# A one-layer decoder step on one core: seventeen products of ones instead of ten ahead of the input's first tile

## The chip, the cores and the metric

The kernel runs on one core of one Trainium2 chip. The metric is the device time of one launch in microseconds (us), less being better. TensorE (PE) multiplies matrices, VectorE (DVE) and ScalarE (ACT) work on elements, GpSimd (POOL) fills constants and starts some transfers, SyncE (SP) starts the large transfers. Each engine runs its own queue of instructions in order and waits on semaphores that the others raise. A row of the trace also tells TensorE's granted clock, which stands at one of two levels: 1.00 is 2.4 GHz, 0.50 is 1.2 GHz.

## The reference

One step of one decoder layer, for 256 prompt tokens and 8 x 4 sampled tokens (288 tokens in all), in float32:

```
u = RMSNorm(x) @ W_in                    # 2048 -> 5632, split between two head groups
x = x + concat([HGRN2(A), SWA(B)]) @ W_out
x = x + SwiGLU(RMSNorm(x))               # 2048 -> 5632 -> 2048
```

The layer also returns the new keys, values and recurrent states. The part that matters here is the very start: `x` (token rows of 2048) must stand transposed (2048 rows in 16 tiles of 128, 288 tokens in columns) and scaled by the norm's weights, before the first product with `W_in` can be made.

## The kernel before

All weights pass through the core in slabs of 1 MB (128 x 2048 float32). SP loads a slab into one of three buffers `raw`; ACT rounds it to `wh` (function `high`, line 646, semaphore `high_done`), DVE forms the rest `wl = raw - wh` (function `low`, line 1002, `low_done`). The activations are split in the same way into `act_h` and `act_l`. PE then makes three products for each slab and each of 16 tiles: `wh*act_h`, `wh*act_l`, `wl*act_h`. For the first slab they are made in an order that follows the arrival of the operands (`passes_as_they_come`): 16 of `wh*act_h` (line 1577), 16 of `wl*act_h` (line 1580), 16 of `wh*act_l` (line 1583). From the second slab on, function `passes` interleaves them (lines 1563, 1564, 1567). There are 44 slabs for `W_in`, 16 for `W_out`, 132 for the feed-forward part.

What comes ahead of the first slab:

- POOL fills `ones` (128 x 128) at line 489. SP starts the transfers of the small constants and of `x` in five pieces: first columns 0 to 1023 of the two prompt blocks, then the whole of the sampled tokens (`x_sample`, 32 rows), then columns 1024 to 2047 of the prompt blocks. The slabs of `W_in` stand behind them in the same queue.
- PE waits for `ones` and makes ten products of `ones` with `ones` (`warm(10)`, line 1527). Their result goes to a bank that is overwritten later and nobody reads it.
- PE waits for the constants and the norm's weights, transposes the weights (line 1532), and makes ten more products of ones.
- PE transposes `x`: for each tile k of 16, three transpositions (line 1513): prompt block 0, prompt block 1, sampled rows. Tile 0 waits for each of the three pieces before its transposition. The results go to six PSUM slots in turn; from tile 6 on, PE waits until tile k-6 has been taken away.
- ACT takes a tile as `act_h[k]` (line 664) and copies the even tiles to `reg_x` (line 667); DVE makes `act_l[k]` (line 1019) and copies the odd ones (line 1023). ACT rounds slab 0 behind tile 9 and slab 1 behind tile 15, DVE makes the rest of slab 0 behind tile 9.
- PE transposes the other parameters (line 1538) and goes on with slab 0.

The order on each engine is the order in which the code is written; there is no planner.

Of the kernel before, what the change touches and what calls it, by code (L numbers as in the profile page):

```python
# [123 lines left out]
def layer_kernel(nc, x_prompt, x_sample, cache_k, cache_v, state_hgrn, norm_mix, w_in, lower_bounds, hgrn_norm,  # L124
# [13 lines left out]
    with ExitStack() as ctx:  # L138
# [1362 lines left out]
        def _(pe):  # L1501
# [23 lines left out]
            def warm(n):  # L1525
                for _ in range(n):
                    mm(mx[:, 0, 0:P], ones, ones, start=True, stop=True)
# [2 lines left out]
            pe.wait_ge(small_in, 16)  # L1530
            pe.wait_ge(gain_in, 16)
            nc.tensor.transpose(acc[3][:, 0:KD], param_rows[0:KD], ident[0:KD, 0:KD]).then_inc(gain_t, 1)
            warm(10)
            for k in range(KD):
                x_transpose(k)
            pe.wait_ge(gain_done, 1)
# [674 lines left out]
```

## Time and profile before

| | us |
|---|---|
| median of 3 runs (1355.39 to 1356.23) | 1355.54 |
| time of the profiled execution | 1357.95 |
| span of the profiled execution, first to last instruction | 1356.1 |
| PE busy in the span | 1348.2 (99%) |
| mean granted clock of TensorE | 0.992 |

The profile is of one execution, whose time is 2.41 us above the median of the runs. The span lacks 1.85 us of that execution's time, which lie outside the first and last instruction. A row of a timeline gives start, duration, engine, line, operation, output<-inputs, shapes and how many instructions of the kind were merged into the row (x20). A product in float32 shows as two matrix instructions, a transposition or a product of rounded operands as one.

### The profile page before, as it was taken

The numbers are of one execution on the slowest core, as the hardware profiler recorded it, in microseconds if no ns is written. First come the engines' busy times: TensorE is split into PE (matmuls) and PEld (weight loads), VectorE is DVE, ScalarE is ACT, GpSimd is POOL, SyncE is SP. The second block draws the span as 40 slices with busy tenths as digits, with TensorE's granted clock in tenths as the row PEclk, the third lists the DMA queues.
The fourth block names the chain that finished last, engine by engine and source line by source line (L and its number), as shares of the span: only waits on it lengthen the run. The fifth ranks groups of instructions, "written<-read, shape, count | busy, mean of one in ns | idle before, by whom it ended". The sixth has DMA issues, their size and how long they took to land.

```text
span 1356.1 us, 25313 instructions
## 1 busy us (share of the span) xinstructions
PE 1348.2 (99%) x11094; PEld 1312.7 (97%) x11094; DVE 772.7 (57%) x1006; ACT 533.5 (39%) x617; POOL 114.3 (8%) x153
## 2 busy tenths in 40 slices
PE   9999999999999999999999999999999999999998
PEld 7999999988999999999999999999999999999998
DVE  5346765699638475455454645555554555555464
ACT  6347975432344244333323333332333333332331
POOL 2010430214100440000000000000000000000000
PEclk7999999999999999999999999999999999999999
DMA  9796545557844546556565555556555555655552
GB/s 276 198 311 172 165 133 149 137 162 203 256 156 143 173 136 186 158 172 168 156 176 166 156 158 184 156 156 173 170 157 162 179 156 168 165 165 156 169 173 71
DMA packets 321082, 231.43 MB, mean 171 GB/s; under 512 B 5175, under 2 KB 292736, under 8 KB 320651
## 3 DMA queue, kind: packets, MB, share of 16 engines
q1 hardware_dynamic: 314768, 206.19, 52.9%
q0 software_dynamic: 6112, 23.59, 5.5%
q8 instruction: 88, 1.44, 0.4%
q14 instruction: 24, 0.19, 0.0%
q10 hardware_dynamic: 90, 0.02, 0.0%
HBM read 219.99 MB, written 14.97 MB: 173 GB/s over the span
## 4 chain that ended last, share of the span: by engine, by line
PE 98%; DMA 1%; ACT 0%; DVE 0%; SPq 0%; issue 0%; DVEq 0%
PE acc L1563 30%; PE acc L1567 30%; PE acc L1564 29%; PE mx L1769 1%; PE mx L1513 1%; DMA reg_qkf<-in_x_sample_dram 1%; PE mx L1681 0%; PE mx L1653 0%; PE mx L1860 0%; PE mx L1668 0%; PE mx L1833 0%; PE acc L1577 0%; PE mx L2085 0%; PE mx L1895 0%; PE acc L1513 0%; PE acc L1580 0%
## 5 line engine op out<-in xcount | busy, mean ns | idle before, releaser
L1563 PE MATMUL acc<-act_h,wh 128*128 128x288 f32 x2208 | 597.0, 299 | 0.0
L1564 PE MATMUL acc<-act_l,wh 128*128 128x288 f32 x2208 | 593.7, 295 | 0.0
L646 ACT ACTIVATE wh<-raw 128x2048 fp32r<-128x2048 f32 x192 | 366.7, 1910 | 241.9 <-PE acc L1567 230.6
L1002 DVE TENSOR_TENSOR wl<-raw,wh 128x2048 fp32r<-128x2048 f32 x192 | 440.1, 2292 | 7.6 <-PE acc L1583 3.9
L1563 PEld LDWEIGHTS acc<-act_h,wh 128*128 128x128 f32 x2208 | 415.5, 188 | 5.9 <-issue 5.0
L1564 PEld LDWEIGHTS acc<-act_l,wh 128*128 128x128 f32 x2208 | 414.7, 188 | 0.1
L1567 PE MATMUL acc<-act_h,wl 128*128 128x288 f32 x2208 | 321.7, 298 | 0.0
L1567 PEld LDWEIGHTS acc<-act_h,wl 128*128 128x128 f32 x2208 | 301.7, 189 | 5.0 <-issue 3.8
L1563 PE MATMUL acc<-mix_h,wh 128*128 128x288 f32 x832 | 228.3, 299 | 0.0
L1564 PE MATMUL acc<-mix_l,wh 128*128 128x288 f32 x832 | 227.7, 295 | 0.0
L1563 PEld LDWEIGHTS acc<-mix_h,wh 128*128 128x128 f32 x832 | 157.1, 189 | 1.7 <-issue 1.7
L1564 PEld LDWEIGHTS acc<-mix_l,wh 128*128 128x128 f32 x832 | 156.2, 188 | 0.0
L1567 PE MATMUL acc<-mix_h,wl 128*128 128x288 f32 x832 | 142.3, 296 | 0.0
L1489 DVE TENSOR_TENSOR reg_x<-acc,reg_x 128x288 f32<-128x288 f32 x176 | 79.2, 455 | 104.7 <-PE acc L1567 104.7
L1567 PEld LDWEIGHTS acc<-mix_h,wl 128*128 128x128 f32 x832 | 120.3, 188 | 0.0
L952 ACT ACTIVATE reg_t<-reg_t 128x288 f32<-128x288 f32 x44 | 19.7, 447 | 185.2 <-DVE reg_t L1454 185.2
L1454 DVE TENSOR_TENSOR reg_t<-acc,reg_t 128x288 f32<-128x288 f32 x44 | 20.1, 457 | 126.3 <-PE acc L1567 126.3
L955 ACT ACTIVATE mix_h<-reg_t 128x288 fp32r<-128x288 f32 x44 | 19.6, 447 | 179.0 <-DVE reg_t L1462 179.0
L1462 DVE TENSOR_TENSOR reg_t<-acc,reg_t 128x288 f32<-128x288 f32 x44 | 20.1, 457 | 119.1 <-PE acc L1567 119.1
L1350 DVE TENSOR_TENSOR reg_x<-acc,reg_x 128x288 f32<-128x288 f32 x32 | 14.3, 453 | 37.5 <-PE acc L1567 37.5
L1456 DVE TENSOR_TENSOR reg_t<-reg_t 128x288 f32<-128x288 f32 x44 | 20.2, 458 | 22.6 <-ACT reg_t L952 22.6
L1466 DVE TENSOR_TENSOR mix_l<-reg_t,mix_h 128x288 fp32r<-128x288 f32 x44 | 20.2, 458 | 22.6 <-ACT mix_h L955 22.6
(284 smaller groups left out, 714.3 us busy)
## 6 DMA issues: line engine op xcount, KB each, us to landing
raw<-in_w_in_dram SPq DMA_DIRECT2D x44, 1024.0 KB, 6.0
raw<-in_w_gate_dram SPq DMA_DIRECT2D x44, 1024.0 KB, 5.6
raw<-in_w_up_dram SPq DMA_DIRECT2D x44, 1024.0 KB, 5.6
raw<-in_w_down_dram SPq DMA_DIRECT2D x44, 1024.0 KB, 5.1
raw<-in_w_out_dram SPq DMA_DIRECT2D x16, 1024.0 KB, 5.3
reg_x<-in_state_hgrn_dram POOLq DMA_DIRECT2D x16, 256.0 KB, 4.8
out_dram<-reg_x POOLq DMA_DIRECT2D x16, 256.0 KB, 3.6
bias_rows<-bias_line POOLq DMA_DIRECT2D x1, 3072.0 KB, 18.3
```

Source lines behind the costliest of these rows:

```text
L646: nc.scalar.activation(wh[:, s % WH, :], raw[:, s % RAW, :], ACT.Copy).then_inc(high_done, 1)
L952: nc.scalar.activation(tmp[:, 2 + t % 2, :], tmp[:, t % 2, :], ACT.Silu).then_inc(gate_silu, 1)
L955: nc.scalar.activation(mix_h[:, FC * (c % 2) + t, :], tmp[:, 4 + t % 2, :], ACT.Copy)\
L1002: nc.vector.tensor_tensor(wl[:, s % WL, :], raw[:, s % RAW, :], wh[:, s % WH, :].bitcast(F32), ALU.subtract).then_inc(low_done, 1)
L1454: nc.vector.tensor_tensor(tmp[:, t % 2, :], ps, rstd2, ALU.mult).then_inc(gate_scaled, 1)
L1456: nc.vector.tensor_tensor(tmp[:, 2 + t % 2, :], tmp[:, 2 + t % 2, :], rstd2, ALU.mult)\
L1462: nc.vector.tensor_tensor(tmp[:, 4 + t % 2, :], ps, tmp[:, 2 + t % 2, :], ALU.mult)\
L1466: nc.vector.tensor_tensor(mix_l[:, slot, :], tmp[:, 4 + t % 2, :], mix_h[:, slot, :].bitcast(F32), ALU.subtract)\
L1489: nc.vector.tensor_tensor(xT[:, m, :], acc[n][:, 0:T], xT[:, m, :], ALU.add)\
L1563: mm(out, w_h[:, i, cols], a_hi[:, place(i), :], start=(i == 0), stop=False)
L1564: mm(out, w_h[:, i, cols], a_lo[:, place(i), :], start=False, stop=False)
L1567: ins = mm(out, w_l[:, i, cols], a_hi[:, place(i), :], start=False, stop=(i == k - 1))
```

## The change

The second batch of products of ones, between the transposition of the norm's weights and the transposition of the first tile of `x`, is made longer by seven. Nothing else differs, and no wait, transfer or buffer is touched.

```diff
             pe.wait_ge(small_in, 16)
             pe.wait_ge(gain_in, 16)
             nc.tensor.transpose(acc[3][:, 0:KD], param_rows[0:KD], ident[0:KD, 0:KD]).then_inc(gain_t, 1)
-            warm(10)
+            warm(17)
             for k in range(KD):
                 x_transpose(k)
```

The order of PE's instructions at the start of the program follows, as a difference (- before, + after; `mx<-reg_a` is the product of ones, `acc<-small,reg_a` the transposition of the norm's weights, `mx<-small,reg_qkf` those of `x`):

```order
 L1527 MATMUL mx<-reg_a 128x128 x10
 L1532 MATMUL acc<-small,reg_a 128x16
-L1527 MATMUL mx<-reg_a 128x128 x10
+L1527 MATMUL mx<-reg_a 128x128 x17
 L1513 MATMUL mx<-small,reg_qkf 128x128 x2
 L1513 MATMUL mx<-small,reg_qkf 128x32
```

Seven products of ones, which are 14 matrix instructions in the trace, now stand ahead of the first transposition of `x`. The order on the other four engines is unchanged.

## Rows read from the trace of the kernel before

**Rows 1.** The page: busy time of the engines, and the chain that ended last
```profile
PE 1348.2 (99%) x11094; PEld 1312.7 (97%) x11094; DVE 772.7 (57%) x1006; ACT 533.5 (39%) x617; POOL 114.3 (8%) x153
PE 98%; DMA 1%; ACT 0%; DVE 0%; SPq 0%; issue 0%; DVEq 0%
```

**Rows 2.** Waits of PE over the whole span: who for whom, us, times, longest
```profile
PE mx L1513 <- DMA reg_qkf<-in_x_sample_dram: 1.3, 1, 1.3
PE mx L1527 <- POOL reg_a L489: 1.0, 1, 1.0
PE mx L2103 <- DVE reg_x L1489: 0.6, 1, 0.6
PE mx L1513 <- DMA reg_qkf<-in_x_prompt_dram: 0.5, 1, 0.5
PE mx L1681 <- ACT reg_x L750: 0.2, 1, 0.2
```

**Rows 3.** Timeline of PE: start us, us, engine, line, operation [idle before <-releaser]
```profile
1.00 4.04 PE L1527 MATMUL mx<-reg_a 128*128 128x128 f32 x20 [1.00 <-POOL reg_a L489]
5.13 2.50 PE L1527 MATMUL mx<-reg_a 128*128 128x128 f32 x20
7.47 0.27 PE L1513 MATMUL mx<-small,reg_qkf 128*128 128x128 f32 x1
8.20 0.33 PE L1513 MATMUL mx<-small,reg_qkf 128*128 128x128 f32 x1 [0.46 <-DMA reg_qkf<-in_x_prompt_dram]
9.85 2.19 PE L1513 MATMUL mx<-small,reg_qkf 32*128 32x32 f32 x10 [1.32 <-DMA reg_qkf<-in_x_sample_dram]
...
22.30 0.33 PE L1538 MATMUL acc<-small,reg_a 43*128 43x43 f32 x1
22.55 4.21 PE L1577 MATMUL acc<-act_h,wh 128*128 128x288 f32 x16
26.56 3.01 PE L1580 MATMUL acc<-act_h,wl 128*128 128x288 f32 x16
29.41 2.29 PE L1583 MATMUL acc<-act_l,wh 128*128 128x288 f32 x16
31.54 0.29 PE L1563 MATMUL acc<-act_h,wh 128*128 128x288 f32 x1
```

**Rows 4.** Stretches: busy us (instructions) of PE, PEld, DVE, ACT, POOL; clock; DMA
```profile
1.30:3.90 2.60, 2.60 (x13) 2.60 (x13) 0.00 (x0) 0.00 (x0) 0.00 (x0) 1.00 0.74 208
5.50:7.40 1.90, 1.90 (x20) 1.90 (x19) 0.00 (x0) 0.07 (x1) 0.00 (x0) 1.00 1.00 281
9.00:10.00 1.00, 0.15 (x1) 0.13 (x1) 0.00 (x0) 0.00 (x0) 0.00 (x0) 1.00 0.94 332
11.00:12.00 1.00, 1.00 (x6) 0.57 (x5) 0.90 (x3) 1.00 (x3) 0.00 (x0) 0.55 1.12 321
11.10:22.30 11.20, 11.20 (x41) 6.05 (x40) 9.44 (x18) 9.94 (x22) 3.45 (x7) 0.50 1.18 287
28.00:29.00 1.00, 1.00 (x8) 1.00 (x8) 0.00 (x0) 1.00 (x2) 0.88 (x3) 0.92 0.83 350
246.00:250.00 4.00, 4.00 (x121) 2.55 (x123) 0.00 (x0) 0.13 (x1) 0.00 (x0) 1.00 1.10 267
250.00:253.40 3.40, 3.40 (x28) 3.06 (x28) 0.00 (x0) 0.60 (x1) 1.97 (x1) 0.50 0.00 0
```

**Rows 5.** Timeline of PE's weight loads for `x`, one row a tile
```profile
9.85 0.37 PEld L1513 LDWEIGHTS mx<-small,reg_qkf 32*128 32x128 f32 x3 [1.51 <-DMA reg_qkf<-in_x_sample_dram]
10.39 0.37 PEld L1513 LDWEIGHTS mx<-small,reg_qkf 32*128 32x128 f32 x3 [0.17 <-issue]
...
14.31 0.53 PEld L1513 LDWEIGHTS mx<-small,reg_qkf 32*128 32x128 f32 x3 [0.33 <-issue]
15.17 0.53 PEld L1513 LDWEIGHTS mx<-small,reg_qkf 32*128 32x128 f32 x3 [0.33 <-issue]
```

**Rows 6.** The chain that ended last, in order of time: start us, us, what
```profile
22.62 4.14 PE acc L1577 x16
...
29.57 2.13 PE acc L1583 x16
```

**Rows 7.** Timeline of PE: products of 288 columns
```profile
35.81 2.30 PE L1567 MATMUL acc<-act_h,wl 128*128 128x288 f32 x16
...
246.26 0.29 PE L1564 MATMUL acc<-act_l,wh 128*128 128x288 f32 x1
...
250.63 3.64 PE L1567 MATMUL acc<-act_h,wl 128*128 128x288 f32 x16
```

**Rows 8.** Timelines of ACT and DVE around slab 0
```profile
19.44 0.49 ACT L664 ACTIVATE act_h<-acc,gains 128x288 fp32r<-128x288 f32 x1
...
20.50 0.52 ACT L664 ACTIVATE act_h<-mx,gains 128x288 fp32r<-128x288 f32 x1
...
22.40 0.50 ACT L664 ACTIVATE act_h<-mx,gains 128x288 fp32r<-128x288 f32 x1
22.80 1.90 ACT L646 ACTIVATE wh<-raw 128x2048 fp32r<-128x2048 f32 x1
...
18.21 0.45 DVE L1023 COPY reg_x<-mx 128x288 f32<-128x288 f32 x1
19.57 2.29 DVE L1002 TENSOR_TENSOR wl<-raw,wh 128x2048 fp32r<-128x2048 f32 x1 [0.92 <-ACT wh L646]
...
24.22 0.93 DVE L1019 SCALAR_TENSOR_TENSOR act_l<-mx,gains,act_h 128x288 fp32r<-128x288 f32 x2
```

**Rows 9.** The issue of slab 0 of `W_in` on SP: time from issue to landing
```profile
L448 SPq DMA_DIRECT2D raw<-in_w_in_dram x1: 787/787/787, 4.1 to 4.1; - x1
DMA to landing us min/median/max: 11.7/11.7/11.7
```

## The prediction

> **What bounds the kernel now.** I read the page first. PE is busy for 1348.2 of 1356.1 us, and the chain that ended last runs over PE for 98% of the span [rows 1]. So the time is the sum of PE's own work: it becomes shorter only if PE idles less, or if its work runs at a better clock. The waits come second. All waits of PE that the trace names add up to 3.6 us, and 1.8 of them stand at the start: 0.5 us for the second prompt block of `x` and 1.3 us for the sampled rows [rows 2]. The third view is PE's timeline over the first 32 us [rows 3]: the second batch of ones begins at 5.13, the first transposition of `x` at 7.47, the second at 8.20, the third at 9.85 with the landing of `x_sample`, and from there PE has no gap. The last view is the granted clock by stretches [rows 4]. PE is nearly idle from 9 to 10 us (0.15 us busy). During the second at 11 to 12 us the clock falls (0.55 on average), it is 0.50 from 11.10 to 22.30, and it comes back in the second from 28 to 29 (0.92, so that it rises at about 28.1). Hence PE works some 17 us at half speed. A tile of `x` takes 0.54 us (9.85 to 10.39) at the full clock and 0.86 us (14.31 to 15.17) at half [rows 5]. Sixteen products of 288 columns take 4.14 us at half and 2.13 us at full by the chain of waits [rows 6], 0.259 and 0.133 us each.
>
> **The products themselves.** The change removes nothing and adds seven products. The ten of the second batch take from 5.13 to 7.47, 0.234 us each [rows 3]. Seven take 7 x 0.234 = 1.64 us and end at 9.11 in place of 7.47. The first two transpositions follow without a wait (0.27 and 0.33 us by their rows, counted in full though they overlap): 9.71. The third can't start before `x_sample` lands at 9.85, as now. So the added work lies wholly in the gap, with 0.14 us to spare, and costs nothing. The cover is the landing of `x_sample`; if it landed earlier than 9.71, each tenth would be paid. Behind PE stand ACT and DVE, which wait for tile 0 as a whole and get it at the same time. No transfer is issued by PE, and none waits for it here.
>
> **What the clock does.** That is the other, less certain term. The clock fell after a stretch in which PE had waited from 7.74 to 8.20 and from 8.53 to 9.85, 1.8 us in all. In the changed kernel PE has dense products of ones until 9.11 and waits for 0.14 us. The clock was full throughout the batch of ones (20 instructions in 1.90 us, against 13 in 2.60 us in the first batch before it had risen; the clock column shows 1.00 there only because the trace holds no earlier step) [rows 4]. From the last dense product to the fall it now takes 11.1 - 7.5 = 3.6 us, and at the second place where it fell (below) about the same: the last product of a slab ends at 246.5, the clock is low at 250.0 [rows 4, 7]. The last dense product moves to 9.1, which gives a fall at 12.7 for the same distance. The transpositions that follow without a gap may hold the clock for longer; I allow the distance once more, 16.3, and take the middle, 14.5. The gain at each:
>
> - At 12.7: 1.6 us more at full, 3.0 tiles in place of 1.9, 1.1 x 0.86 = 0.95 us won by the transpositions.
> - At 14.5: 3.4 us, 6.3 tiles in place of 4.0, 2.3 x 0.86 = 2.0 us won. PE would be done with the parameters at 20.6 and not at 22.55.
> - At 16.3: 5.2 us, 9.6 tiles in place of 6.0, 3.6 x 0.86 = 3.1 us, as far as DVE follows.
>
> Does something else hold PE back? Tile 15 needs DVE's copy of tile 9, done at 18.66; tile 15 would start at about 19.4. Slab 0 is rounded by 19.5 (the rest of it starts at 19.57), `act_h[15]` is made at 22.90, the rest of slab 0 at 21.86, and the last `act_l` at 25.15 [rows 8]. Even if ACT and DVE gained nothing, PE needs `act_h[15]` at 24.4, the rest of slab 0 at 24.7 and the last `act_l` at 27.5 or later. So PE keeps the 2.0 us up to the first slab.
>
> With 2.0 us won, the first slab's products begin at 20.6 and 16 at half speed end at 24.7. Now the rise decides. (a) If it stays at 28.12: 3.4 us at half give 13.2 of the next 16 products, 2.8 x 0.133 = 0.4 us more, then 2.13: 30.65 in place of 31.54, a gain of 0.9 us. (b) If it comes as long after the first dense product as now (28.12 - 22.55 = 5.6 us), at 26.2: 5.8 products at half, 10.2 x 0.133 = 1.36, then 2.13: 29.7, a gain of 1.85 us. (c) If it comes as long after the first dense product as at the second place, where the products begin at 250.63 and the clock is back at 253.4, 2.8 us [rows 4, 7], it comes at 23.4: 10.8 products at half, 5.2 x 0.133 = 0.7, then twice 2.13: 28.4, a gain of 3.2 us. With the fall at 12.7 about half of these remain, 0.5 to 1.6; with the fall at 16.3 some half more. I take (b), 1.85 us, near the middle of 0.9 and 3.2.
>
> **A second place.** The clock is also 0.50 from 250.0 to 253.4, behind 4.00 us in which PE was fully busy with small products [rows 4]. Sixteen products take 3.64 us there and 2.30 us elsewhere [rows 7], a price of 1.3 us. When everything lies 2 us earlier this may vanish or not: 0 to 1.3 us. I put it at zero in the sum and keep it for the range.
>
> The profiled execution took 1357.95 us, so it would come to 1356.1. It stood 2.41 us above the median of the runs, though; half-speed stretches are the one thing in the trace that could differ that much, so the median may lack part of what is to be won. I still take the same 1.85 us off the median: 1355.54 - 1.85 = 1353.7.
>
> **Two rules of the Trainium skill.** The record shows PE 100% busy from 11.10 to 22.30, 11.20 us, with the clock at 0.50 all the time, and fully busy from 246 to 250 with the clock at 0.50 behind it [rows 4]. The Trainium skill's page "TensorE: Matmul & The Clock Gate", section "What's actually happening", says that the gate follows how busy the array has been recently. If "busy" were what the rows call busy, the clock would have come back among the transpositions; the trace doesn't bear that reading out, and transpositions seem to weigh little. By that reading the sum would be that of rival 2.
>
> The same page of the Trainium skill, in the same section, warns that the number of slow products varies from run to run with the moment at which a kernel starts, and advises not to fit to a count of them. No row here can show it, since there is one execution. By that rule the sum for the median would be near nothing, rival 1.
>
> **The rivals.**
>
> 1. *The median doesn't move.* The clock falls where it did, since seven products aren't enough to hold it, or it falls and rises at other moments in most executions, so that the gap mattered only in the profiled one. For it: the 2.41 us between profile and median. Against it: the clock fell right behind the only idle stretch at the start, and three runs within 0.84 us leave little room for a clock that changes at other moments each time. Time: 1355.5, with up to 0.3 us either way.
> 2. *The clock stays full throughout the transpositions.* ACT then sets the pace: tile 0 at 10.2, two tiles in 1.06 us (19.44 to 20.50) [rows 8], ten tiles by 15.5; slab 0 lands at 4.1 + 11.7 = 15.8 [rows 9], is rounded by 17.7, six tiles more by 21.0. PE ends the 16 first products at 21.1, and 4.26 us later, at 25.4, the slab: 6.1 us won, 1349.4. Against it: 11.20 us of pure transpositions never brought the clock back.
> 3. *Slower: the seven are made at half speed.* A product of ones takes 0.40 us before the rise (2.60 us for 13 instructions, two a product) [rows 4]. Were the clock still low in the second batch, it would last until 5.13 + 17 x 0.40 = 11.9, two transpositions go to 12.5, and tile 0 is 2.6 us late; ten would have ended in time. Time: 1355.54 + 2.6 = 1358.1. It decides from the first product that is slow beyond the 0.14 us of room, at 0.17 us each. Against it: in the profile the clock was up before the second batch.
>
> **How the numbers follow.** A change within 0.2% (2.7 us) is about what a measurement of this kernel can't tell from none. Chances: the forecast case 0.58 (gain 0.5 to 3.2 us, with the second place up to 4.5), rival 1 0.33, rival 2 0.03, rival 3 0.06. Of the forecast case about 0.15 lies beyond 2.7 us, where (c) holds or the second place is added. With rival 2: faster 0.19, same 0.76, slower 0.05 (a part of rival 3 is smaller than 2.7 us). The range reaches from 1351.4 (the forecast case with 4.1 us) to 1356.0 (rival 1 with a little loss); about 0.15 lies outside.
>
> **What the profile would show.** PE's second batch is 34 instructions from 5.13 to about 9.1, the wait for the second block is gone, and that for `x_sample` is under 0.3 us. The granted clock is 1.00 until 12.7 or later, tiles come every 0.54 us until then, L1577 begins near 20.6 and L1563 near 29.7. The forecast is wrong if the clock falls at 11.1 again, if the second batch ends after 9.5, or if PE starts to wait for ACT or DVE among the tiles.

## The result

The changed kernel takes 1351.91 us (median of 8 runs, 1351.41 to 1353.1), the kernel before 1356.2 us in the same measurement (median of 8 runs, 1355.39 to 1357.93). The ratio is 0.9972, with a 95% interval of 0.9959 to 0.9984: faster by 0.28%, which is clear of no change. The forecast of 1353.7 us was 1.8 us too high, inside the range (1351.4 to 1356.0), but the step that gave it was not the one that took place.

The page of the changed kernel, busy time of the engines:

```profile
PE 1342.5 (99%) x11108; PEld 1309.2 (97%) x11108; DVE 772.2 (57%) x1006; ACT 532.6 (39%) x617; POOL 116.3 (9%) x153
```

PE makes 14 more matrix instructions than in [rows 1] and is busy for 5.7 us less: the same work ran at a better clock. The span is 1350.0 us where it was 1356.1, and the mean granted clock 1.000 where it was 0.992. PE's timeline over the start, to be laid beside [rows 3]:

```profile
1.00 4.62 PE L1527 MATMUL mx<-reg_a 128*128 128x128 f32 x20 [1.00 <-POOL reg_a L489]
5.55 0.23 PE L1532 MATMUL acc<-small,reg_a 16*128 16x16 f32 x1
5.72 4.06 PE L1527 MATMUL mx<-reg_a 128*128 128x128 f32 x34
9.62 2.18 PE L1513 MATMUL mx<-small,reg_qkf 128*128 128x128 f32 x12
...
18.23 0.25 PE L1538 MATMUL acc<-small,reg_a 43*128 43x43 f32 x1
18.42 2.43 PE L1577 MATMUL acc<-act_h,wh 128*128 128x288 f32 x15
21.14 0.40 PE L1577 MATMUL acc<-act_h,wh 128*128 128x288 f32 x1 [0.29 <-ACT act_h L664]
21.39 2.28 PE L1580 MATMUL acc<-act_h,wl 128*128 128x288 f32 x16
23.50 2.30 PE L1583 MATMUL acc<-act_l,wh 128*128 128x288 f32 x16
25.64 0.29 PE L1563 MATMUL acc<-act_h,wh 128*128 128x288 f32 x1
```

The products of ones and the transpositions follow each other without a gap. The transpositions end at 18.2 (22.3 before), slab 1 begins at 25.64 (31.54 before): 5.9 us earlier. The stretch of transpositions, for [rows 4] (busy us and instructions of PE, weight loads, DVE, ACT, POOL; granted clock; DMA):

```profile
11.10:18.20 7.10, 7.10 (x40) 4.37 (x40) 6.48 (x16) 6.97 (x16) 3.45 (x7) 1.00 1.19 296
246.00:250.00 4.00, 4.00 (x98) 3.58 (x97) 1.49 (x6) 2.03 (x3) 2.91 (x2) 1.00 0.00 0
250.00:253.40 3.40, 3.40 (x28) 3.40 (x27) 3.40 (x5) 1.40 (x6) 0.00 (x0) 1.00 0.02 5
```

The clock is 1.00 all through them; forty instructions take 7.10 us, against 11.20 us for 41 in [rows 4]. The second half-speed stretch, at 250 us, is absent as well (1.3 us by [rows 7]). Part of this goes into new waits. PE's waits over the span:

```profile
PE mx L1527 <- POOL reg_a L489: 1.0, 1, 1.0
PE mx L1611 <- ACT reg_t L685: 0.8, 1, 0.8
PE mx L2103 <- DVE reg_x L1489: 0.6, 1, 0.6
PE mx L1769 <- issue: 0.4, 1, 0.4
PE acc L1577 <- ACT act_h L664: 0.3, 1, 0.3
```

The waits for `x` of [rows 2] are gone. PE now waits 0.3 us for ACT's last tile, as it no longer runs slowly enough to be always behind, and 0.8 us for ACT at the squares of a head group (line 1611). 5.9 won at the start, 1.3 at 250 us, 0.8 and 0.4 given back at lines 1611 and 1769 make 6.0 of the 6.1 us between the spans.

So the two profiles differ by 6.1 us and the two medians by 4.3. Two questions are left: why these differ, and what holds the clock.

### The profile page after: what moved, and what is told of

The parts are those of the page before. It is cut to its first block, busy times and chain, and to the rows that moved or that the text cites. A ratio compares the mean times of both kernels' runs of the same rounds, so it can differ in the third digit from the quotient of the medians.

```text
span 1350.0 us, 25341 instructions
## 1 busy us (share of the span) xinstructions
PE 1342.5 (99%) x11108; PEld 1309.2 (97%) x11108; DVE 772.2 (57%) x1006; ACT 532.6 (39%) x617; POOL 116.3 (9%) x153
## 4 chain that ended last, share of the span: by engine, by line
PE 96%; DMA 2%; ACT 1%; DVE 0%; issue 0%; SPq 0%; DVEq 0%
PE acc L1563 30%; PE acc L1567 30%; PE acc L1564 29%; DMA raw<-in_w_in_dram 2%; PE mx L1769 1%; PE mx L1681 0%; PE mx L1653 0%; PE mx L1860 0%; PE mx L1668 0%; PE mx L1833 0%; PE mx L2085 0%; PE mx L1895 0%; PE mx L1810 0%; PE mx L1698 0%; PE mx L1705 0%
```

## Experiments

Each set of three or four kernels ran with the kernel before on the same chip, 12 executions a kernel and 29 or 35 of the kernel before; the three sets ran on three different chips. Every execution tells its mean granted clock. I sort them in two groups: 0.998 and more, called held, and 0.997 and less, called fallen (most of these have 0.992 to 0.995). In the first two sets of the kernel before no value lies between 0.995 and 0.998; in the third three of 29 do (0.996 once, 0.997 twice, 1354.83 to 1357.02 us), and they are counted as fallen. That the line tells a clock held at the start from one that fell there is shown by the profiled executions alone, each of which agrees with it. A held execution can still have a short stretch at half speed elsewhere.

| kernel | filler, where | held | median us | median held | median fallen |
|---|---|---|---|---|---|
| before, set 1 | 10 products | 8 of 35 | 1355.95 | 1351.97 | 1356.71 |
| nine transpositions | 10 + 9 transpositions | 6 of 12 | 1354.57 | 1352.43 | 1356.97 |
| 17, then an idle wait | 17 | 0 of 12 | 1359.53 | | 1359.53 |
| 24 products | 24 | 12 of 12 | 1352.73 | 1352.73 | |
| 14 products | 14 | 7 of 12 | 1353.44 | 1353.13 | 1356.94 |
| before, set 2 | 10 | 8 of 35 | 1355.84 | 1351.01 | 1356.38 |
| fifteen transpositions | 10 + 15 transpositions | 10 of 12 | 1352.46 | 1352.35 | 1354.10 |
| six in the middle of tile 0 | 10 + 6 | 11 of 12 | 1352.70 | 1352.62 | 1355.14 |
| seven in the first batch | 17 + 10 | 12 of 12 | 1352.74 | 1352.74 | |
| 17 products again | 17 | 12 of 12 | 1352.35 | 1352.35 | |
| before, set 3 | 10 | 7 of 29 | 1355.83 | 1351.16 | 1356.21 |
| 27 products | 27 | 11 of 12 | 1354.36 | 1354.17 | 1358.27 |
| 12 products | 12 | 3 of 12 | 1355.84 | 1350.68 | 1356.14 |
| 12 ahead, 5 in the middle | 12 + 5 | 11 of 12 | 1353.08 | 1352.94 | 1353.87 |

The first measurement of the changed kernel adds 8 of 8 held. This answers the first question. **The kernel before is a mixture**: in 23 of 99 executions the clock holds and the median time is 1351 to 1352, in 76 it falls and the median time is 1356.2 to 1356.7, about 5 us more. The change doesn't make a held execution faster. It makes nearly all executions held ones. The share of fallen ones, 76 of 99, times 5.0 us is 3.8 us, less what the products themselves cost. The first measurement of the kernel before has no clock beside its eight times, but all are 1355.39 us or more, above every held execution of the table's kernel before (1353.87 at most): by their times all eight are fallen, which explains why its difference, 4.3 us, is larger than in the sets.

### Filler of another kind

```diff
             warm(10)
+            for _ in range(9):
+                nc.tensor.transpose(mx[:, 0, 0:P], ones, ident)
             for k in range(KD):
```

> The gap ahead of the sampled rows is filled with nine transpositions of the ones tile (0.17 to 0.20 us each at the full clock, about 1.6 us) in place of the seven products of ones. Theory A (an idle gap lets the clock fall, any work that fills it holds the clock): as the changed kernel, clock 1.00 throughout, 1352 us, L1563 begins near 25.6. Theory B (only dense products of ones hold it; transpositions weigh too little): the clock falls near 11 us as before, 1355.5 to 1356.5 us. Theory C (chance: clock steps lie elsewhere in each execution): a mixture, 1352 to 1356.

Held in 6 of 12, ratio 0.9993 (0.9974 to 1.0011), not told apart from before. This was undecided: nine transpositions were shorter than I had counted. PE's timeline of this kernel (line 1535 is the filler), in an execution whose clock held:

```profile
5.24 2.50 PE L1527 MATMUL mx<-reg_a 128*128 128x128 f32 x20
7.58 1.15 PE L1535 MATMUL mx<-small,reg_a 128*128 128x128 f32 x9
8.56 0.57 PE L1513 MATMUL mx<-small,reg_qkf 128*128 128x128 f32 x2
10.00 1.87 PE L1513 MATMUL mx<-small,reg_qkf 32*128 32x32 f32 x10 [0.88 <-DMA reg_qkf<-in_x_sample_dram]
```

They took (8.56 - 7.58) / 9 = 0.109 us each and left 0.88 us idle. So fifteen were tried in the next set, `range(15)` in place of `range(9)`:

> In the last set nine transpositions took only 0.109 us each and left 0.9 us of idling; the clock held in 6 of 12 executions. Fifteen of them behind the ten products fill the gap to about 9.1 us, as seven products of ones do. Theory A (only the idle time ahead of the landing matters, whatever the work is): held in all or nearly all executions, median 1352. Theory B (the kind of work matters, dense products hold the clock and transpositions hold it less well): still a mixture, a quarter or more of the executions with the clock at 0.995 or less and 1355 to 1359 us.

Held in 10 of 12, ratio 0.9984 (0.9971 to 0.9998). Filling the gap with transpositions does nearly what filling it with products does; the two others have a mean clock of 0.996 and 1354.0 and 1354.2 us, so they were at half speed for less time than most fallen executions of before; where, no profile shows. Theory A gives the main effect. Whether the kind of work matters a little besides is left open by 10 of 12 against 20 of 20.

### An idle wait behind the seventeen

```diff
                     if k % 8 == 0 and k // 8 < len(x_in[j]):
                         pe.wait_ge(x_in[j][k // 8], 16)
+                    if k == 0 and j == 2:
+                        pe.wait_ge(x_in[1][1], 16)
```

> The changed kernel with seventeen products, but the third transposition of tile 0 also waits for the last piece of x (lands near 12.1 us), so that PE idles some 2.2 us behind the products. Theory A: the clock falls in the idle stretch or right behind it and the gain is lost: about 1356.2 plus up to 2.2 for the later tile 0, 1356.5 to 1358.5 us, clock 0.50 during most of the transpositions. Theory B (seventeen dense products are what holds the clock): clock 1.00, only the direct 2.2 us are lost: about 1354 us.

1359.53 us, ratio 1.0025 (1.0012 to 1.0038); no execution of 12 held. Stretches of this kernel:

```profile
11.00:12.00 1.00, 0.00 (x0) 0.00 (x0) 0.00 (x0) 0.00 (x0) 0.00 (x0) 1.00 1.15 315
12.00:13.00 1.00, 0.86 (x6) 0.64 (x6) 0.00 (x0) 0.54 (x2) 0.33 (x1) 1.00 1.19 291
13.00:14.00 1.00, 1.00 (x5) 0.49 (x4) 0.64 (x2) 1.00 (x3) 1.00 (x3) 0.52 1.19 289
14.00:24.00 10.00, 10.00 (x37) 5.44 (x36) 8.12 (x15) 8.68 (x20) 2.12 (x5) 0.50 1.02 244
```

PE idles for 1.88 us until 12.14, the clock falls in the second from 13 to 14 (0.52 on average), and ten microseconds of transpositions without a gap don't bring it back. Seventeen products don't protect against a gap behind them. The time is above my upper end (1358.5): it lies 2.8 us above the fallen executions of before (1356.71), of which 2.3 are the lateness of tile 0 (12.14 against 9.85). In its profile PE has two more waits that the kernel before doesn't have [rows 2], 0.8 us together, which are enough for the rest:

```profile
PE mx L1613 <- ACT reg_t L685: 0.5, 1, 0.5
PE mx L1771 <- issue: 0.3, 1, 0.3
```

### The same delay without idling

To take the delay apart from the clock, `warm(27)` in place of `warm(17)`:

> Twenty-seven products: the batch and two transpositions end near 12.1 us, so tile 0 is as late as in the kernel with the wait for the last piece of x (third transposition at 12.14), but PE isn't idle. Theory A: held in all executions; only the direct price of the later tile 0 is paid, at most 2.2 us: 1353 to 1354.5 us, 5 to 6 us below the 1359.5 of the kernel with the idle wait. If the lateness of tile 0 itself made the 1359.5: as slow, 1358 or more.

Tile 0's third transposition comes later still than in the kernel with the wait (12.45 + 0.33 = 12.8 against 12.14), and yet the time is 1354.36 us, 5.2 us less, in another set whose kernel before has nearly the same median (1355.83 against 1355.95); 11 of 12 held where I had expected all (the other has 0.997). The kernel with the wait differs in that PE idles. So the idle stretch costs 5 us through the clock, and lateness alone costs 2.0 us (1354.36 - 1352.35, in two sets) for some 2.2 us of lateness against seventeen (12.8 against 10.6 in the profile shown below). Its ratio to before is 0.9993 (0.9981 to 1.0005): with ten products more, the kernel can't be told apart from the one before.

### More and fewer products

`warm(24)`, `warm(14)` and `warm(12)`:

> Twenty-four products in the second batch. All theories: the clock stays full. The batch ends 7 x 0.112 x 2 = 1.6 us after that of seventeen, at 10.7 to 11.3, so tile 0 is complete about 1.2 to 1.5 us later. If ACT and the landing of slab 0 at 15.9 had room, less of it is lost; by the rows ACT takes up slab 0 without a wait behind tile 9, so I expect 1.0 to 1.5 us above seventeen: 1353.0 to 1353.5 us.

> Fourteen products: four of the seven, so 0.9 us of the 1.8 us of idling stay. Theory A: about half the idling; the clock is held in many executions but not in all: 1352 to 1356 us with a wide spread. Theory B (a count of dense products): nearly as seventeen, 1352 to 1353 us. If the gap must vanish entirely, 1356 us.

> Twelve products, 0.45 us of the gap filled. Shares of held executions so far: ten 8 of 35 twice, fourteen 7 of 12, seventeen 20 of 20. I expect the share to grow with the filled time: 4 to 6 of 12, median near 1355.5. As few as ten gives would say that there is a threshold between twelve and fourteen.

Twenty-four: held in 12 of 12, 1352.73 us, 0.4 to 0.8 above seventeen where I had expected 1.0 to 1.5; ratio 0.998 (0.9966 to 0.9993). Fourteen: 7 of 12, ratio 0.9988 (0.9971 to 1.0005). Twelve: 3 of 12 where I had expected 4 to 6, ratio 1.0002 (0.9986 to 1.0019), the share of ten. The share of held executions rises from a quarter at ten and twelve to about half at fourteen and to all at seventeen, 20 of 20. With 12 executions a share is known to about a quarter, so where exactly it bends isn't settled, but it rises with how much of the gap is filled, and the executions of a kernel differ. In the profiled execution of twelve products the clock held and PE's products and transpositions had no wait for `x` at all (the weight load of the third transposition waited 0.2 us), as the first batch had run slowly for longer and the second began at 5.79 rather than at 5.13:

```profile
1.00 4.64 PE L1527 MATMUL mx<-reg_a 128*128 128x128 f32 x20 [1.00 <-POOL reg_a L489]
5.57 0.28 PE L1532 MATMUL acc<-small,reg_a 16*128 16x16 f32 x1
5.79 3.38 PE L1527 MATMUL mx<-reg_a 128*128 128x128 f32 x24
9.00 2.22 PE L1513 MATMUL mx<-small,reg_qkf 128*128 128x128 f32 x12
```

Twenty-four instructions took 3.21 us from start to start of the next, 0.134 each, where the second batch before had 0.117: the clock rose only after the second batch had begun. The moment of the first rise moves from one execution to the next, and with it how wide the gap is. The other end of the gap moves too. SP issues the transfer of `x_sample` at 2.1 us in every profile, and it lands 7.2 us later in the one of twelve products, 7.7 in the one of before and 8.3 in the one of the last kernel below, in this order (KB, us to landing):

```profile
reg_qkf<-in_x_sample_dram SPq DMA_DIRECT2D x1, 256.0 KB, 7.2
reg_qkf<-in_x_sample_dram SPq DMA_DIRECT2D x1, 256.0 KB, 7.7
reg_qkf<-in_x_sample_dram SPq DMA_DIRECT2D x1, 256.0 KB, 8.3
```

These are two visible reasons for the mixture. How much each has to do with it isn't shown, as there is one profile of each kernel and none of a held execution of the kernel before.

### Other places for the same seven

Ahead of the norm weights' transposition (17 + 10), and in the middle of tile 0:

```diff
                     if k % 8 == 0 and k // 8 < len(x_in[j]):
+                        if k == 0 and j == 2:
+                            for _ in range(6):
+                                mm(acc[0][:, 0:P], ones, ones, start=True, stop=True)
                         pe.wait_ge(x_in[j][k // 8], 16)
```

> The seven products are added to the first batch, ahead of the norm weights' transposition (17 + 10). PE ends the second batch at the same time, as the constants have landed by then. Theory A and B: held in all executions, 1352 as the changed kernel. If the count in the second batch is what matters: as before, 1356.

> Ten products in the second batch as before, and six products of ones between the second and the third transposition of tile 0, just ahead of the wait for the sampled rows. They fill the longer of the two waits (1.3 us), the shorter (0.5 us) stays. Theory A and B: held in most executions (8 or more of 12), median 1352 to 1353.5. If it were a matter of the place ahead of tile 0, for instance of when tile 0 is ready, the share stays at 8 of 35 and the median at 1356.

Held in 12 and 11 of 12; ratios 0.9984 (0.9972 to 0.9996) and 0.9983 (0.997 to 0.9996). No difference between the places shows in 12 executions. In the profile of 17 + 10, 0.6 us of the wait for the sampled rows is left, and the clock holds:

```profile
9.09 0.38 PE L1513 MATMUL mx<-small,reg_qkf 128*128 128x128 f32 x2
10.09 1.87 PE L1513 MATMUL mx<-small,reg_qkf 32*128 32x32 f32 x10 [0.62 <-DMA reg_qkf<-in_x_sample_dram]
```

The gap need not vanish entirely.

### The changed kernel again, and a candidate

> The changed kernel once more, on the chip and beside the runs of before of this set: held in all 12 executions (clock 0.998 or more), median 1352 against 1356 of before with its mixture. A fall in one or two executions would say that seventeen lies at the edge.

1352.35 us, ratio 0.9979 (0.9965 to 0.9993), held in 12 of 12. Its profiled execution is the longest of its 12 (1355.97 us, span 1354.2), and its waits show what varies among held ones:

```profile
PE mx L1611 <- ACT reg_t L685: 2.0, 1, 2.0
PE acc L1564 <- issue: 1.3, 1, 1.3
```

The first of them in its timeline, where PE stands still for ACT's squares:

```profile
95.36 0.91 PE L1611 MATMUL mx<-reg_t,small 128*32 128x288 f32 x4 [2.04 <-ACT reg_t L685]
```

This wait fits the same account at another place of the program. Behind it the clock is at half for about 3.5 us:

```profile
95.00:95.60 0.60, 0.24 (x2) 0.14 (x4) 0.59 (x1) 0.58 (x2) 0.00 (x0) 1.00 1.15 343
95.60:99.10 3.50, 3.50 (x16) 2.91 (x13) 2.99 (x3) 2.41 (x3) 0.00 (x0) 0.51 0.78 192
99.10:100.00 0.90, 0.90 (x9) 0.90 (x8) 0.90 (x1) 0.87 (x2) 0.00 (x0) 1.00 1.02 304
```

In the first profile of the changed kernel PE waits 0.75 us for ACT at this place and the clock stays at 1.00. The mean clock of this execution is 0.998, so it counts as held: the clock did hold at the start.

The same timeline at its start shows that seventeen can overshoot; PEld is the weight load:

```profile
10.22 1.46 PE L1513 MATMUL mx<-small,reg_qkf 128*128 128x128 f32 x8
10.53 0.37 PEld L1513 LDWEIGHTS mx<-small,reg_qkf 32*128 32x128 f32 x3 [0.17 <-issue]
```

The third transposition follows the second weight load at 10.53, where it stood at 9.85 before. The candidate splits them, `warm(12)` ahead of tile 0 and five products between its second and third transposition:

> A candidate: twelve products ahead of tile 0 (they fill the wait for the second block) and five between its second and third transposition (they fill the wait for the sampled rows). Seventeen in all, but two transpositions come before five of them, so nothing stands between the landing and the third transposition but the end of a product. Held in all executions; if seventeen in one place cost anything where the clock rises late (its third transposition came at 10.5 us in one profile), this saves up to 0.5 us: 1351.5 to 1352.5.

1353.08 us, held in 11 of 12 (the other 0.997), ratio 0.9981 (0.9969 to 0.9994). I had expected 1351.5 to 1352.5 and all twelve held. It doesn't beat seventeen in one place. No kernel tried did. In the candidate's profile `x_sample` landed late, at about 10.4 us (2.1 + 8.3), and the third transposition ran at 10.49, so it was the landing and not the filler that set tile 0 there.

## Why the prediction was right in its range and wrong in its step

**The products lie in the gap.** Right in kind, a little too tight. They were to end at 9.11 with 0.14 us to spare. In the changed profile they end at 9.62 (the first batch was slower, the second began at 5.72), and `act_h[0]` starts at 10.27 where it started at 10.20: 0.1 us lost, 0.7 in the execution above (10.87). Among held executions of the second set seventeen products take 1352.35 and ten 1351.01, 1.3 us apart; the held ten of the first set, on another chip, have 1351.97, 0.4 less than seventeen. That the products aren't free where the clock would have held anyway is one reading. I can see 0.1 to 0.7 of the 1.3 us in tile 0. The other is a selection that no run excludes: the held executions of ten may be those in which `x_sample` lands early, as in the profile of twelve products (7.2 us, 1350.55 us in all), and would then be shorter on that account too.

**The clock.** Here the step failed. I took the fall to be put off, to 14.5, with a rise at 26.2 and 1.85 us won. In fact it doesn't fall at all, and PE gains 5.9 us at the start. That is rival 2, to which I gave 0.03 and for which the working was nearly exact: it put the end of the first slab at 25.4, and slab 1 began at 25.64, with PE waiting for ACT's last tile. (Its time of 1349.4 took 6.1 us off the median of three; taken off the profiled execution's 1357.95, the 6.1 give 1351.85, and the changed kernel's profiled execution took 1351.8, since the 1.3 us won at 250 us and the 1.2 us of new waits nearly cancel.) What misled me is the sentence that "11.20 us of pure transpositions never brought the clock back". It is true, and the kernel with the idle wait shows it again, but it says only that transpositions don't raise a low clock. It says nothing on whether they hold a high one: they do, 7.10 us of them in the changed kernel. I took evidence for one direction as evidence for both. The distance of 3.6 us from the last dense product to the fall, on which I built the 12.7, 14.5 and 16.3, doesn't give the moment of a fall: in the changed kernel 8.8 us of transpositions (9.62 to 18.42) stand behind the last dense product, and the clock is 1.00 all through them.

**The reading of the rule.** The Trainium skill's page "TensorE: Matmul & The Clock Gate" (section "What's actually happening") lets the gate follow recent activity. I set it aside on the strength of the transpositions at half speed. For falls at the start it was the better guide: an idle gap is what lets the clock fall (held in 0 of 12 with a new gap, in 20 of 20 without one). For the second place, before 250 us, where PE was fully busy with small products when the clock fell [rows 4], it stays as little explained as before.

**The profile and the median.** I noted that the profiled execution stood 2.41 us above the median and that the median might lack part of the gain. That was so, in another way: a quarter of the executions had no fall to lose. It doesn't explain the 2.41 us, as the three runs, 1355.39 and more, were fallen ones by their times too; the 1.3 us of the stretch at 250 us may be a part of them. The second warning of that page of the Trainium skill, that slow products vary from run to run, agrees with the traces: the second batch begins at 5.13 to 5.79 in the profiles with ten products in the first. But it doesn't follow that the median stays, which is what I made of it in rival 1. A change can move the share of the good executions. Against rival 1 I also held that three runs within 0.84 us leave no room for such variation; 35 runs of the same kernel span 1350.8 to 1360.3. Three runs say little on a mixture: with 76 of 99 fallen, three of three are fallen in nearly half of all cases (0.77 x 0.77 x 0.77 = 0.46, an estimate).

**The sum.** That the time fell in the range is luck. Two errors partly offset each other: the gain of a fallen execution was sized at 1.85 in place of about 5 us (5.9 at the start of the profiled one), and it was taken off every execution rather than off three in four. Only the low end of the range, made for a late fall, an early rise and the second place, reached the measured time. Computed from what the runs show, 0.77 x 5.0 less 0.4 to 1.3 for the products gives 2.5 to 3.4 us. That is a difference of means; in the second set the means are 1355.28 and 1352.71, 2.6 us apart (the medians 3.5). In the first measurement, with all eight executions of before fallen, 5.0 less 0.4 to 1.3 gives 3.7 to 4.6, and 4.3 was measured.

**The second place** was left out of the sum and it vanished in the changed profile, but it seems to be chance as well: with fourteen products, in an execution whose clock held at the start, it is low near there again (0.72 on average from 244 to 250 us, the row below). **Rival 3** didn't occur, save for the small overshoot where the clock rises late.

```profile
244.00:250.00 6.00, 6.00 (x104) 5.42 (x106) 0.50 (x3) 1.51 (x3) 2.91 (x2) 0.72 0.04 10
```

## What to carry to other kernels

Where PE waits for its first input, what follows can run at half speed for much longer than the wait lasts: here two waits of 1.8 us together cost 5 us in three executions of four. Fill such a gap up to the landing and not much beyond it: products of ones held the clock in 20 of 20, transpositions in 10 of 12, and with ten products more no gain could be told from none. Evidence that some work doesn't raise the clock is no evidence that it can't hold it. And when a profiled execution stands off the median, look at the mean clock of every execution before sizing a gain: a share may be what moves.

## What the runs showed that I had not expected

- TensorE's clock depended on where it stood: transpositions without a gap kept it at 1.00 for 7.10 us (2.4 GHz) and left it at 0.50 for 10.00 us (1.2 GHz) when it had fallen ahead of them.
- Behind a wait of 2.04 us at line 1611 the clock was 0.50 for about 3.5 us; behind one of 0.75 us at the same place it stayed at 1.00 (one execution each).
- One kernel, one input, one core at a time on three chips: 23 of 99 executions near 1351 us and 76 near 1356, told apart by the mean granted clock.
- The same transfer, issued at 2.1 us, took 7.2 to 8.3 us to land in the profiles, and PE's gap ends with it.
- A transposition of 128 x 128 float32 in a run of like ones takes 0.109 us start to start, against 0.223 us for a product of the same shape (two matrix instructions; the transpositions of `x` begin at 12.45 with 27 products and at 10.22 with 17, and 2.23 / 10 is 0.223).
